# A two-layer decoder step on one core: value weights in pieces, halved head weights, two state buffers swapped, a normaliser stored as rows

## The reference

```python
v = proj[..., 2 * W_A:3 * W_A].reshape(B, T, H_A, DH_A)            # layer 0: values
...
q = jnp.einsum('bthd,hde->bhte', ca_h, w_q.astype(F32))            # layer 1, head by head
k = jnp.einsum('bthd,hde->bhte', ca_h, w_k.astype(F32)) * (DH_C ** -0.5)
v = jnp.einsum('bthd,hde->bhte', xm.astype(F32).reshape(B, T, H_C, DH_C), w_v.astype(F32))
...
num = w_inter[..., None] * jnp.einsum('bhtd,bhde->bhte', q, C) + jnp.einsum('bhts,bhse->bhte', s, v)
den = w_inter * jnp.einsum('bhtd,bhd->bht', q, n) + jnp.sum(s, axis=-1)
C_new = decay[..., None, None] * C + jnp.einsum('bhsd,bhse->bhde', k * w_s[..., None], v)
n_new = decay[..., None] * n + jnp.einsum('bhs,bhsd->bhd', w_s, k)
```

## Time and profile before

| | |
|---|---|
| three timed runs, median | 2160.86 us |
| profiled execution, its own time | 2151.39 us |
| span of the profile (first to last instruction) | 2149.7 us |
| mean granted clock of TensorE | 0.959 of full speed |
| TensorE busy / VectorE / ScalarE / GpSimd | 91% / 52% / 31% / 6% |
| DMA | 282.67 MB, mean 131 GB/s |

### The profile page before, as it was taken

One profiled execution on the slowest core, in us unless ns is written; L12 is line 12 of the kernel. 1 busy time (PEld: TensorE's weight loads), 2 busy tenths in 40 slices (PEclk: granted clock), 3 DMA queues, 4 the chain that ended last, 5 costly groups with the idle time before them and its releaser, 6 DMA issues. The chain is left out here.

```text
span 2149.7 us, 28420 instructions
## 1 busy us (share of the span) xinstructions
PE 1960.9 (91%) x11413; PEld 1623.5 (76%) x11413; DVE 1119.9 (52%) x1815; ACT 675.0 (31%) x1185; POOL 120.7 (6%) x199
## 2 busy tenths in 40 slices
PE   4999998787775989999999799999999999989998
PEld 4999997555543869999999796588678669555886
DVE  5241112888523344544434457837866865775542
ACT  4111111777422223322222332232232232234221
POOL 0000000000212000000000001200110110100000
PEclk7999998999987999999999999999999999989999
DMA  5111112300476314675676424653662661867552
GB/s 158 40 43 52 50 51 69 91 1 1 153 232 253 99 48 85 126 128 125 157 138 207 157 81 166 200 151 127 212 196 82 213 199 59 244 207 251 163 160 85
DMA packets 174647, 282.67 MB, mean 131 GB/s; under 512 B 15683, under 2 KB 110727, under 8 KB 173402
## 3 DMA queue, kind: packets, MB, share of 16 engines
q1 hardware_dynamic: 146533, 179.54, 29.7%
q0 software_dynamic: 27840, 100.80, 14.3%
q10 hardware_dynamic: 144, 0.52, 0.1%
HBM read 185.70 MB, written 95.31 MB: 131 GB/s over the span
## 5 line engine op out<-in xcount | busy, mean ns | idle before, releaser
L1445 PE MATMUL pre_ps<-x_xh,pre_wh 128*128 128x358 f32 (+1 forms) x792 | 261.0, 330 | 6.7 <-DVE pre_wl L1567 6.7
L1446 PE MATMUL pre_ps<-norm_xl,pre_wh 128*128 128x358 f32 (+1 forms) x792 | 259.6, 328 | 0.0
L1447 PE MATMUL pre_ps<-x_xh,pre_wl 128*128 128x358 f32 (+1 forms) x792 | 258.8, 327 | 0.0
L426 PE MATMUL proj_ps<-x_xe,proj_wh 128*128 128x368 f32 x480 | 161.0, 335 | 4.8 <-DVE proj_wl L539 4.8
L428 PE MATMUL proj_ps<-x_xe,proj_wl 128*128 128x368 f32 x480 | 159.5, 332 | 0.0
L427 PE MATMUL proj_ps<-lo_xl,proj_wh 128*128 128x368 f32 x480 | 159.1, 331 | 0.0
L1445 PEld LDWEIGHTS pre_ps<-x_xh,pre_wh 128*128 128x128 f32 x792 | 150.3, 190 | 8.2 <-DVE pre_wl L1567 7.2
L1447 PEld LDWEIGHTS pre_ps<-x_xh,pre_wl 128*128 128x128 f32 x792 | 150.5, 190 | 0.0
L1446 PEld LDWEIGHTS pre_ps<-norm_xl,pre_wh 128*128 128x128 f32 x792 | 150.3, 190 | 0.0
L539 DVE TENSOR_TENSOR proj_wl<-all_w,proj_wh 128x1024 fp32r<-128x1024 f32 x24 | 29.2, 1225 | 193.2 <-ACT proj_wh L501 193.2
L1914 PE MATMUL head_ps<-head_cl,head_wh 128*128 128x358 f32 (+1 forms) x384 | 125.2, 326 | 0.0
(11 more groups left out here) (447 smaller groups left out, 4244.1 us busy)
## 6 DMA issues: line engine op xcount, KB each, us to landing
head_Cs<-in_state_C POOLq DMA_DIRECT2D x20, 1024.0 KB, 9.0
out_C_s<-head_Cs POOLq DMA_DIRECT2D x19, 1024.0 KB, 5.1
x_xnT<-in_cache_sb_k SPq DMA_DIRECT2D x64, 256.0 KB, 3.3
all_w<-in_w_in_c SPq DMA_DIRECT2D x32, 512.0 KB, 9.4
all_w<-in_w_in_a SPq DMA_DIRECT2D x24, 512.0 KB, 3.8
paged_vp<-in_cache_sb_v POOLq DMA_DIRECT2D x48, 256.0 KB, 4.2
head_Cs_top<-in_state_C POOLq DMA_DIRECT2D x12, 1024.0 KB, 9.0
out_C_s<-head_Cs_top POOLq DMA_DIRECT2D x12, 1024.0 KB, 4.8
```

What stands on the lines that cost most here:

```text
L426: pe.matmul(out, wh[:, t % 2, k, :], xh[:, k, c0:c1], start=(k == 0), stop=False)
L1445: pe.matmul(out, wh[:, t % 2, k, :], xh[:, k, c0:c1], start=(k == 0), stop=False)
L1446: pe.matmul(out, wh[:, t % 2, k, :], xl[:, k, c0:c1], start=False, stop=False)
L1447: last = pe.matmul(out, wl[:, t % 2, k, :], xh[:, k, c0:c1], start=False, stop=(k == KD - 1))
```

## The change

It has six parts, A to F.

A. The value weights of `even_input` are converted in pieces of two k slices (VK = 2, 128x256 a tile): ACT makes piece after piece, DVE follows, and `values` waits inside its first row tile, before each second k, for that piece only. For the second half a piece is one slice pair of both tiles.

B. The conversions of w_k and w_v in `heads` are halved (128x1024): w_k at c = 3 and 4, w_v at c = 5 and 6.

C. At step 7 `low_x` of the next head's second x tile moves behind `prompt_states`, and ACT's `high_x` of the first tile moves from the head's start to before `decayed(7)`.

D. `high_c` and `low_c` move from value tiles n = 4 to 7 to n = 5 to 8, and the wait for the stored C moves from k = 0 to k = 2.

E. The normaliser of the prompt is transposed by TensorE (one matmul, 4x128 into a PSUM bank, in `query_sums`, m = 0), copied by DVE to `n_rows`, and stored by one DMA of four rows of 512 bytes. In the last head, SP stores it after `small_done`.

F. For heads 0 to 2 the slots are 0, 1, 2, 0, 1, 2, 1, 0: state 6 goes into slot 1 and state 7 into slot 0. The last head keeps the old order. The load of state 6 then waits for the store of state 4, issued just before it, and the load of state 7 for the store of state 3.

```diff
             def values(h):
-                pe.wait_ge(wl_done, NF + 2 * h + 2)
                 for i in range(NT + 1):
...
                     for k in range(KD):
+                        if i == 0 and k % VK == 0:
+                            pe.wait_ge(wl_done, NF + 1 + VP * h + k // VK + 1)
...
+            def high_pieces(tiles, count, freed):
+                for t in tiles:
+                    act.wait_ge(w_in[t % WR], 16 * (t // WR + 1))
+                act.wait_ge(freed, count)
+                for k in range(0, KD, VK):
+                    for t in tiles:
+                        last = act.activation(wh[:, t % 2, k:k + VK], w[:, t % WR, k:k + VK], ACT.Copy)
+                    last.then_inc(wh_done, 1)
...
-            for t in range(NF + 1, len(TILES)):
-                high(t)
+            high_pieces((NF + 1,), turn_of(*TILES[NF - 1]) + 1, full)
+            high_pieces((NF + 2, NF + 3), 3 * PAIRS + NT + 1, side_full)
...
+            def low_pieces(tiles, h):
+                for n in range(VP):
+                    k = slice(VK * n, VK * (n + 1))
+                    dve.wait_ge(wh_done, NF + 1 + VP * h + n + 1)
+                    for t in tiles:
+                        last = dve.tensor_tensor(wl[:, t % 2, k], w[:, t % WR, k], wh[:, t % 2, k].bitcast(F32), ALU.subtract)
+                    last.then_inc(wl_done, 1)
...
+CS_ORDER = (0, 1, 2, 0, 1, 2, 1, 0)
+CS_LAST_ORDER = (0, 1, 2, 0, 1, 2, 0, 1)
...
                         if b + CSR - 1 < B:
-                            pool.wait_ge(cs_out[(b - 1) % CSR], cs_count(e, b - 1))
-                            load(b + CSR - 1)
+                            a, n = ((b, 6) if b == 4 else (b - 2, 7)) if e < HC - 1 and b in (4, 5) else (b - 1, b + CSR - 1)
+                            pool.wait_ge(cs_out[cs_slot(e, a)], cs_count(e, a))
+                            load(n)
...
-                with nc.allow_non_contiguous_dma(reason="512 words"):
-                    for m in range(KH):
-                        pool.dma_start(d["out_n_p"].rearrange("l b h (k p o) -> (l b h) p k o", p=P, o=1)[e, :, m],
-                                       nall[:, m, NT - 1:NT]).then_inc(n_out, 16)
+                pool.dma_start(d["out_n_p"].rearrange("l b h (k p) -> (l b h) k p", p=P)[e], n_rows[:, :]).then_inc(n_out, 16)
...
             def query_sums(e, m):
                 one = const[:, C_ONE:C_ONE + 1]
                 if m == 0:
+                    pe.wait_ge(n_done, e + 1)
+                    pe.transpose(ps[0:KH, 5, 0:P], nall[:, :, NT - 1], const[:, C_ID:C_ID + P]).then_inc(nrows_full, 1)
...
             def high_c(e, k):
                 if k == 0:
                     act.wait_ge(c_in, 16 * (e + 1))
-                    if e >= 1:
-                        act.wait_ge(c_out, 16 * e)
+                if k == CH_OVER_C and e >= 1:
+                    act.wait_ge(c_out, 16 * e)
...
-                    if n >= KH and n < 2 * KH:
-                        high_c(e, n - KH)
+                    if n >= NV - KH:
+                        high_c(e, n - (NV - KH))
...
+                    if c == NT - 1 and e + 1 < HC:
+                        high_x(e + 1, 0)
                     decayed(e, c)
                     if e + 1 < HC:
-                        if c == 4:
-                            high_wk(e + 1)
-                        elif c == 6:
-                            high_wv(e + 1)
+                        if c in (3, 4):
+                            high_wk(e + 1, c - 3)
+                        elif c in (5, 6):
+                            high_wv(e + 1, c - 5)
...
             def sample_norms(e):
                 dve.wait_ge(nsum_full, e + 1)
+                if e >= 1:
+                    dve.wait_ge(n_out, 32 * e)
+                dve.wait_ge(nrows_full, e + 1)
+                dve.tensor_copy(n_rows[:, :], ps[0:KH, 5, 0:P])
...
                         low_x(e + 1, 0)
-                        low_x(e + 1, 1)
                     numerator(e, c)
                     prompt_states(e, c)
+                    if c == NT - 1 and e + 1 < HC:
+                        low_x(e + 1, 1)
                     moments(e, c)
```

More of the change, by code:

```diff
@@ L156 @@
 WR = 3
+VK = 2
+VP = KD // VK
 ECH = ((0, 368), (368, 736), (736, T))
@@ L607, in _ @@
             save_keys(PAIRS - 1, 2)
-            low(NF + 1)
+            low_pieces((NF + 1,), 0)
             save_values(0)
-            low(NF + 2)
-            low(NF + 3)
+            low_pieces((NF + 2, NF + 3), 1)
             save_values(1)
@@ L1079, with cs_slot @@
 CSR = 3
-CS_USES = [len(range(j, B, CSR)) for j in range(CSR)]
+CS_ORDER = (0, 1, 2, 0, 1, 2, 1, 0)
+CS_LAST_ORDER = (0, 1, 2, 0, 1, 2, 0, 1)
+CS_USES = [CS_ORDER.count(j) for j in range(CSR)]
+assert CS_USES == [CS_LAST_ORDER.count(j) for j in range(CSR)]
+def cs_slot(e, b):
+    return (CS_LAST_ORDER if e == HC - 1 else CS_ORDER)[b]
 def load_gates(nc, sp, d, w, w_in):
@@ L1732, in heads @@
         assert s.place["Cs"] + 8 * QM + 8 * XT <= s.place["ks"] and s.place["t1"] >= s.place["Cs"] + 8 * QM + 4 * XT
+        CH_OVER_C = 2
+        assert s.place["Cs"] + 4 * QM + 4 * XT * CH_OVER_C <= s.place["C"]
         ps = s.ps("ps", [P, 8, BANK])
@@ L1758, in rows_at, with cs @@
             return (P, seq(i)) if i < NT else (SQ, slice(0, SQ))
-        def cs(b):
-            return Cs_top[:, :, :] if b % CSR == 0 else Cs[:, b % CSR - 1]
+        def cs(e, b):
+            j = cs_slot(e, b)
+            return Cs_top[:, :, :] if j == 0 else Cs[:, j - 1]
         def cs_count(e, b):
-            return 16 * (CS_USES[b % CSR] * e + b // CSR + 1)
+            j = cs_slot(e, b)
+            return 16 * (CS_USES[j] * e + sum(cs_slot(e, a) == j for a in range(b + 1)))
         def s_unit(b, m):
@@ L1769, in heads, with halves @@
         LAST = B - 1
+        def halves(h):
+            return slice(KH // 2 * h, KH // 2 * (h + 1))
         def c_unit(c, m):
@@ L1995, in sample_parts @@
                     pe.wait_ge(nsum_done, e + 1)
-                pe.wait_ge(cs_in[b % CSR], cs_count(e, b))
+                pe.wait_ge(cs_in[cs_slot(e, b)], cs_count(e, b))
                 for k in range(KH):
-                    last = pe.matmul(ps[NS * k:NS * (k + 1), 7, :], qm[:, k, b, :], cs(b)[:, k, :], start=(b == 0), stop=(b == B - 1))
+                    last = pe.matmul(ps[NS * k:NS * (k + 1), 7, :], qm[:, k, b, :], cs(e, b)[:, k, :], start=(b == 0), stop=(b == B - 1))
                 if b == B - 1:
@@ L2135, in high_wk @@
                     act.wait_ge(p_full, NJ * (e - 1) + KH)
-                act.activation(wh[:, 1], w[:, 1], ACT.Copy).then_inc(whk, 1)
+                act.activation(wh[:, 1, halves(h)], w[:, 1, halves(h)], ACT.Copy).then_inc(whk, 1)
             def high_wq(e):
@@ L2206, in _ @@
                 if e == 0:
-                    high_wk(0)
+                    high_wk(0, 0)
+                    high_wk(0, 1)
                 for n in range(NV):
@@ L2264, in low_w, with low_half @@
                 dve.tensor_tensor(wl[:, slot], w[:, slot], wh[:, slot].bitcast(F32), ALU.subtract).then_inc(done, 1)
+            def low_half(slot, high, done, e, h):
+                dve.wait_ge(high, 2 * e + h + 1)
+                dve.tensor_tensor(wl[:, slot, halves(h)], w[:, slot, halves(h)], wh[:, slot, halves(h)].bitcast(F32), ALU.subtract).then_inc(done, 1)
             def sample_values(e):
@@ L2449, in _ @@
                         low_x(e, n + 2)
-                    if n >= KH and n < 2 * KH:
-                        low_c(e, n - KH)
+                    if n >= NV - KH:
+                        low_c(e, n - (NV - KH))
                     low_v(e, n)
```

53 lines of the change are left out of this document (25 added, 28 removed).

## The result

The changed kernel takes 2127.66 us (median of 4 runs, 2124.93 to 2128.14) against 2159.49 for the kernel before (4 runs, 2152.2 to 2163.3): ratio 0.9864, 95% interval 0.9843 to 0.9885. Three of these four runs of the kernel before are the ones that stood ahead of the forecast. Timed again (5 runs) in turn with 11 runs of the kernel before it took 2126.67 against 2151.74: 0.988, interval 0.986 to 0.990. In every later set the kernel before is at 2150 to 2152 us too, so the change is worth 25 us, and not the 32 of the first comparison; the forecast was 18.7, and its 2142 stands 14 us too high. The profiled execution has a span of 2123.2 us, 26.5 less than before.

What follows compares the result with a forecast made beforehand. TensorE, busy 91% of the span, was taken to bound the kernel. Terms -4.5 - 5.3 - 2.9 - 8.4 + 1.6 + 0.8 = -18.7 us took the median from 2160.86 to 2142; range 2135 to 2149.

Steps and rivals of the forecast that it cites:

- The rival that gave the timed runs more of the removed waits: The 9.47 us between timed runs and profile may lie in the same DMA waits and go too: 2133; chance 0.06.
- E's transposes: One added TensorE transpose with 128 columns per head costs 0.15 to 0.2 us each: +0.8 in four heads.
- A: Value projection: waits for low weights shrink 1.5 and 1.5 us, plus 1.5 of slow clock regained: -4.5 (-2.5 to -5.2).
- B: Steps 3 to 6: each half of 1.23 us hides below 1.39 of cover; six times 0.88 saved: -5.3 (0 to -5.3).
- C: Step 7, three heads: the 1.51 us wait loses 1.07 each, 0.28 excess stays, +0.3 for the moved tile: -2.9.
- The heads' starts: Heads 1 to 3, first value tile to first projection: stretches fall to TensorE's work, -8.4 us (0 to -8.4).
- D's own cost: Project 0 waits 0.4 us per head for the last low part of c: +1.6 in four heads (0 to 4).
- F: Load of state 6, now behind state 4's store, is ready at 1367.8, 1.0 us before TensorE's read: 0.
- c in the place of C: Head 1's start: c's transfer still lands late, the stretch keeps 4.3 us or more of its loss: 2146 to 2151; chance 0.16.
- Halves not hidden: Each half weight puts VectorE behind TensorE in four steps, so that gain is 0: 2147; chance 0.08.
- load of state 6 late: Heads 0 to 2: TensorE's read of state 6 waits 8.5 us each, plus 4.5 of clock: 2172; chance 0.05.
- no change: Each wait is only replaced by the next; less than a quarter of the sum stays: about 2158; chance 0.05.

Runs made afterwards that it cites:

- E alone: Kernel before with only the normaliser stored as four rows instead of 512 small writes, in all heads: 2137.88 us against 2151.16, ratio 0.9943.
- D alone: Kernel before with only the copies of c one value tile later and the wait for the stored C at k = 2: 2146.66 us, ratio 0.9977.

## Why the prediction was wrong

Its direction held, and so did most of its mechanisms; the reason given for the clock in A and the way D and E work together did not. The time left the range for two other reasons, the base that the sum started from and a place that it left out. Point by point:

- **The base.** "I carry the difference over unchanged" is the step that failed most, 9 of the 14 us. The difference of 9.47 between the timed runs and the profile was three runs on one occasion. From the profile's 2151.39, where later runs put the kernel before, the same sum gives 2132.7, and the range 2135 to 2149 becomes 2125.5 to 2139.5, which holds 2127.66. The rival that gave the timed runs more of the removed waits (2133) is not borne out: against the kernel before at 2151.74 the gain is 25 us all the same.
- **E in the last head had no term.** The sum followed the small writes to the starts of heads 1 to 3 only, although the description of part E names the store in the last head too. They cost 3.7 us there in the kernel before, shown in the trace by removing them alone.
- **E's transposes**, priced at 0.8, cost nothing that the traces show: with E alone, a head takes from its first projection to its first update of C the same 51.6 us as before.
- **A** was 4.5. The two waits fell by 3.2, where 3.0 was priced. The 1.5 of clock was counted as gained because the new wait is near one that left the clock alone; that reason failed. The profile of the result has the gain. The second profile of the same kernel, with the same waits, runs 3.4 us at the low level behind the first of them. So the term came out right in the first of the two by luck. From the last matmul ahead of the values to the first of attention, the five profiles of before and its variants take 64.1 to 67.0 us and the nine with pieces 59.6 to 62.6: A is 4.9 by their means. The Trainium skill ("VectorE: DVE Perf Modes", section "The TRN2 errata — SBUF-src ops pay a fixed extra latency per instruction") states a fixed cost per instruction, and by its formula for fp32 four pieces of 256 columns would take 1.70 us, an estimate. The trace has the cost, but a smaller one: the four pieces take VectorE 1.43 us, the whole took 1.23. It is hidden behind the matmuls of the pieces.
- **B** was 5.3; the steps of the changed kernel show 0.9 less, six times: right, and the cover is as worked out. Undone it gives 6.0 in the trace.
- **C** was 2.9; found 3.5, since the excess of 0.28 that I left in step 7 is not there; the later second tile costs 0.1 to 0.2 a head, as allowed.
- **The heads' starts** were 8.4, found 8.7 to 9.2 where D's own cost is not in it; that cost was 1.6, found 1.7. The reason was half right: I let E and D work together, and each alone does all of it.
- **F** was 0, and is. The load of state 6 lands earlier than I allowed, 5.6 us instead of 9.0.
- **The rivals.** c in the place of C: c did land in 16.9 us with D alone, and ScalarE's wait of 1.10 us for it was not long enough to reach TensorE. Halves not hidden, load of state 6 late, no change: none of them came.
- **The range and the chances.** The bounds given for A to E do not add up to the range: their best ends, with the 0.8 of E's transposes, come to 21.3 us, 2139.6 from 2160.86 and not 2135. The four cases said to be faster add up to 0.90, not to 0.89 with a part of the fifth.

From the traces: 4.9 (A) + 5.4 (B) + 3.5 (C) + 8.7 (heads' starts) + 3.7 (last head) - 1.7 (D) = 24.5; by the timed runs 25.1. What lies between them is within what single profiles differ by.

## What to carry to other kernels

When a change removes something that loads the DMA queues, list every place where it is issued, in each loop's last round too, and price the transfers beside it there, not only those behind it. When two edits aim at one wait, do each alone: here either was enough, and the second then costs what it costs. A forecast for one execution is best set against the profile's own time, unless many timed runs show another.

## What the runs showed of the hardware

512 writes of four bytes, 2 KB in all, on SyncE's queue in the last head slowed 1 MB transfers on GpSimd's: with rows in their place the store takes 5.0 us instead of 11.8, the load 8.7 instead of 13.5. Their own time to landing does not tell of that. At the start of head 1, behind the store of C on the same queue, the four DMAs of small writes took 13.1 us, and the one DMA of rows in the changed kernel took 11.0 there (DMA issues, KB each, us to landing; first before, then after):

```profile
out_n_p<-head_nall POOLq DMA_DIRECT2D x4, 0.5 KB, 13.1
```

```profile
out_n_p<-head_n_rows POOLq DMA_DIRECT2D x1, 2.0 KB, 11.0
```

A load of 1024 KB behind a finished store landed in 5.6 us, beside a store that was under way in 8.8 to 9.0. Waits of one length were followed by either level of TensorE's clock. The wait of 1.99 us at the values was followed by the full level in four profiles and by 3.4 us at a granted clock of 0.50 in five, and the 3.33 us before the change by a clock of 1.00. The wait of 2.25 us in the last head of before was followed by matmuls of 0.63 instead of 0.40 us, at a granted clock of 0.50, for some 3 us, and one of 1.8 us in the changed kernel with small writes there by none (timeline of TensorE in the last head of before):

```profile
1867.18 0.57 PE L1914 MATMUL head_ps<-head_vl,head_kwh 128*128 128x512 f32 x1
1867.54 0.63 PE L1915 MATMUL head_ps<-head_vh,head_kwl 128*128 128x512 f32 x1
```
